# A stick-breaking and a softmax attention loop: values stationary, output turned, gate turned, probabilities scaled by GpSimd

## Chip, core and metric

One NeuronCore of a Trainium2 chip runs the whole program. The metric is the device time of one execution in microseconds; the median of three runs stands for a kernel. TensorE, VectorE (DVE), ScalarE (ACT), GpSimd (POOL) and SyncE (SP) each work through a queue of their own and wait for each other through semaphores.

## What is computed

Two transformer blocks on 256 tokens of 1024 features, all in float32. The first has a pooling mixer (layer 0) and a stick-breaking attention with 16 heads of 64 (layer 1); the second has a layer with 8 MLA heads (96-wide keys, 64-wide values) and 8 MoBA heads of 64 that here are plain causal softmax, an S5 layer, and two squared-ReLU MLPs. The parts that matter:

```
# stick-breaking attention, heads of 64, mask s < t
logits   = q k^T / 8
log_keep = where(mask, log_sigmoid(-logits), 0)
later    = reverse_cumsum(log_keep) - log_keep
a        = where(mask, exp(log_sigmoid(logits) + later), 0)
o        = a v
x        = x + (o * silu(z)) @ b_w_out        # q, z = split(rms_norm(x) @ b_w_in)
# softmax attention, 16 heads, mask s <= t
p        = softmax(where(mask, q k^T, -inf))
x        = x + concat_heads(p v) @ w_o
```

## The kernel before

Tokens lie on the partitions in two tiles of 128 (`NT` = 2). A dense product needs both operands with the contracted features on the partitions, so `turn` transposes activations on TensorE (L728) into `hT`, and each float32 factor is split into a high part and a low rest: ScalarE writes the high part (`turned_high`, `whi` in `fill`), VectorE the low part (`turned_low`, `wlo` in `fill`). A product is three matmuls per block of 128 features (`three`, L735 to L737): activations stationary, 512 columns of weights moving. The MLP of layer 0 has it the other way round (`hidden`, L1060 to L1064): weights stationary, 256 token columns moving.

Weights come through a ring of two blocks, loaded by SP in the order of `loads`; SP waits for `low_made` of the block two before. They are split in halves of 128 x 2048 into three parts of `whi` and `wlo`; `refill(name, half)` in the queues of ScalarE and VectorE makes the half that stands three halves behind `name`.

The eight banks of PSUM are given out by a plan written by hand (`plan`, `soft_plan`): each use of a bank is a unit with the engine that empties it ("a" ScalarE, "v" VectorE). `begin(unit)` makes TensorE wait until the previous unit of that bank is emptied. Each engine's queue is written out in the order of the code; nothing is scheduled at run time.

Layer 1 runs its products in the order `k`, `v`, `q`, `zb` (the gate z), with the turns of k and q between them. `v`, `q`, `k` and the gate lie token by token (`v_tok` and so on); the gate is scaled by the rows' `rstd` and put through Silu by ScalarE as it leaves PSUM (L1281).

The stick loop goes over pairs of heads, j = 0 to 10, with `LAG` = 2. In iteration j TensorE does `stick_logits(j)` (L885 to L891, two heads on 64-row tiles), at j = 2 three products `ple` (L844), then `stick_logs` of pair j-2 (L898 to L903: the reverse cumulative sum as products with triangular matrices, added into the bank that holds the logits), then `stick_values` of pair j-3 (L912 to L914: the weights of a head as the stationary operand, 64 columns of values moving). `logits` and `loga` of head i use bank i % 6. ScalarE does, head by head, Abs (L1465), Exp (L1466), the Exp of the finished log weights (L1473) and Ln (L1480), each on 128 x 384. VectorE does softplus (L2085), the high part (L2090) and the low part (L2094) of it, and multiplies each four heads' output by the gate (L2100, into `h`). After the loop come `ple(1, 1, 1)`, the turn of `h` (unit "o1"), ScalarE's and VectorE's split of it, and the product `b_out`.

The softmax loop goes over i = 0 to 19 with `AHEAD` = 3. TensorE computes the scores of head i (`mla_scores`, L978 and L979; `moba_scores` for two heads at once, L992 and L994; the masks L968 and L969), turns the probabilities of head i-3 (`probs_turned`, L1003) and multiplies those of head i-4 with the values (`soft_values`, L1014 to L1016). VectorE does the maxima (L2209, L2210), copies the turned probabilities (L2229), and for each four heads the reciprocals of the sums and the scaling of the output (`soft_out`, L2217 and L2218); four pieces of the weights' low part (`refill_piece`, L1739) stand in its queue for i = 10 to 13. ScalarE does the two Exp of a head with their sums (L1537, L1539). The turned keys and queries of the MoBA heads come through bank 7. After the loop come the turn "o2" of `h`, its split, and the product `w_o`. GpSimd does nothing in this loop; behind it, it clears and stores `taps` and begins the S5 multiplies (L2425 to L2430).

## Time and profile before

| | us |
|---|---|
| median of three runs | 868.62 (868.02 to 869.25) |
| span of the profiled execution, first to last instruction | 866.2 |
| its own whole time | not on the page; the span is the figure to compare |
| TensorE busy | 851.7 (98% of the span), 5659 instructions |
| weight loads of TensorE | 737.0 (85%) |
| VectorE busy | 591.9 (68%) |
| ScalarE busy | 441.4 (51%) |
| GpSimd busy | 117.3 (14%) |
| granted TensorE clock | 1.000 over the whole span |

Durations of matmuls overlap (their ends are modelled), so the distance between starts is what a matmul costs, not its duration. A float32 product shows as two records, a product of split parts as one. The chain that ended last names what the end waited for at each moment; 2% of idle time of TensorE is spread over many short waits.

### The profile page before, as it was taken

To read this page: it belongs to the slowest core of one execution; us is meant where nothing else is said; L and a number is where in the kernel's file an instruction comes from. 1 tells how busy PE (TensorE), PEld (TensorE's weight loads), DVE (VectorE), ACT (ScalarE), POOL (GpSimd) and SP (SyncE) were. 2 spreads that over 40 slices of the span, in tenths; PEclk is the share of its full clock that TensorE was granted. 3 is DMA by queue.
4 is the path that set the end of the run, shared out by engine and by line. 5 is a ranking of instruction groups with operands and counts; after the bars stand their busy time and mean duration, and the time that the engine had idled before them with its cause. 6 is when DMAs were issued, how large, how long until landed. Compare 5 with 4: busy or idle time off the path is not lost.

```text
span 866.2 us, 13480 instructions
## 1 busy us (share of the span) xinstructions
PE 851.7 (98%) x5659; PEld 737.0 (85%) x5659; DVE 591.9 (68%) x738; ACT 441.4 (51%) x591; POOL 117.3 (14%) x74
## 2 busy tenths in 40 slices
PE   8999999999999999999999999999989999999998
PEld 7887888888788887888988889997868999999996
DVE  5684677666756678888788788786975655555553
ACT  6644466556953656754553446443164644444441
POOL 0100001111000004123144344540000000000000
PEclk9999999999999999999999999999999999999999
DMA  9927645555004436226455565556976465555621
GB/s 332 372 75 246 239 146 196 194 194 184 11 22 154 160 98 244 97 97 210 157 198 167 207 231 195 209 190 140 282 265 235 151 210 182 188 190 194 194 98 48
DMA packets 68405, 155.96 MB, mean 180 GB/s; under 512 B 3145, under 2 KB 6954, under 8 KB 68346
## 3 DMA queue, kind: packets, MB, share of 16 engines
q1 hardware_dynamic: 65312, 146.80, 50.1%
q0 software_dynamic: 2224, 7.67, 2.6%
q10 hardware_dynamic: 810, 0.63, 0.5%
q8 instruction: 45, 0.74, 0.3%
q14 instruction: 14, 0.11, 0.0%
HBM read 146.70 MB, written 7.34 MB: 178 GB/s over the span
## 4 chain that ended last, share of the span: by engine, by line
PE 91%; DVE 6%; ACT 2%; issue 1%; DMA 0%; ACTq 0%; DVEq 0%
PE bank L735 19%; PE bank L736 19%; PE bank L737 19%; PE bank L1062 7%; PE bank L1064 7%; PE bank L1060 7%; PE bank L728 3%; PE bank L844 2%; PE bank L834 1%; PE bank L946 1%; PE bank L885 1%; DVE pT L1826 1%; PE bank L1133 1%; PE bank L1122 1%; DMA vrows<-in_vecs 0%
## 5 line engine op out<-in xcount | busy, mean ns | idle before, releaser
L1725 DVE TENSOR_TENSOR wlo<-ring,whi 128x2048 fp32r<-128x2048 f32 (+1 forms) x103 | 251.7, 2449 | 135.3 <-ACT whi L1334 135.0
L1334 ACT ACTIVATE whi<-ring 128x2048 fp32r<-128x2048 f32 (+1 forms) x104 | 198.4, 1909 | 208.3 <-PE bank L737 143.2
L735 PE MATMUL bank<-whi,hT 128*128 128x512 f32 (+1 forms) x512 | 201.6, 394 | 3.2 <-DVE wlo L1955 1.4
L737 PE MATMUL bank<-whi,hT 128*128 128x512 f32 (+1 forms) x512 | 198.8, 388 | 0.0
L736 PE MATMUL bank<-wlo,hT 128*128 128x512 f32 (+1 forms) x512 | 198.7, 388 | 0.0
L1060 PE MATMUL bank<-hT,whi 128*128 128x256 f32 x512 | 145.3, 284 | 0.0
L1062 PE MATMUL bank<-hT,whi 128*128 128x256 f32 x512 | 144.9, 283 | 0.0
L1064 PE MATMUL bank<-hT,wlo 128*128 128x256 f32 x512 | 144.8, 283 | 0.0
L735 PEld LDWEIGHTS bank<-whi,hT 128*128 128x128 f32 x512 | 96.1, 188 | 25.0 <-issue 2.7
L737 PEld LDWEIGHTS bank<-whi,hT 128*128 128x128 f32 x512 | 96.1, 188 | 19.6
L736 PEld LDWEIGHTS bank<-wlo,hT 128*128 128x128 f32 x512 | 96.2, 188 | 19.0 <-issue 0.5
L1060 PEld LDWEIGHTS bank<-hT,whi 128*128 128x128 f32 x512 | 98.2, 192 | 0.6
L1062 PEld LDWEIGHTS bank<-hT,whi 128*128 128x128 f32 x512 | 98.2, 192 | 0.5
L1064 PEld LDWEIGHTS bank<-hT,wlo 128*128 128x128 f32 x512 | 98.2, 192 | 0.0
L735 PE MATMUL bank<-whi,hidT_hi 128*128 128x512 f32 x224 | 88.0, 393 | 0.0
L736 PE MATMUL bank<-wlo,hidT_hi 128*128 128x512 f32 x224 | 87.4, 390 | 0.0
L737 PE MATMUL bank<-whi,hidT_lo 128*128 128x512 f32 x224 | 87.2, 389 | 0.0
L1720 DVE SCALAR_TENSOR_TENSOR wlo<-ring,vcols,whi 128x512 fp32r<-128x512 f32 x64 | 43.8, 745 | 20.6 <-ACT whi L1330 20.6
L1330 ACT ACTIVATE whi<-ring,vcols 128x512 fp32r<-128x512 f32 x64 | 40.9, 711 | 19.3 <-PE bank L737 17.0
L735 PEld LDWEIGHTS bank<-whi,hidT_hi 128*128 128x128 f32 x224 | 42.1, 188 | 9.7 <-issue 1.2
L737 PEld LDWEIGHTS bank<-whi,hidT_lo 128*128 128x128 f32 x224 | 42.1, 188 | 9.0
L736 PEld LDWEIGHTS bank<-wlo,hidT_hi 128*128 128x128 f32 x224 | 42.1, 188 | 8.2
(296 smaller groups left out, 1026.9 us busy)
## 6 DMA issues: line engine op xcount, KB each, us to landing
ring<-in_w_ff SPq DMA_DIRECT2D x64, 1024.0 KB, 5.3
ring<-in_ple_gate_w SPq DMA_DIRECT2D x8, 1024.0 KB, 5.0
ring<-in_w_kv SPq DMA_DIRECT2D x8, 1024.0 KB, 5.0
ring<-in_b_w_in SPq DMA_DIRECT2D x8, 1024.0 KB, 5.0
ring<-in_a_w_in SPq DMA_DIRECT2D x7, 1024.0 KB, 13.1
ring<-in_w_in SPq DMA_DIRECT2D x6, 1024.0 KB, 5.8
ring<-in_w_glu SPq DMA_DIRECT2D x6, 1024.0 KB, 10.1
ring<-in_a_w_out SPq DMA_DIRECT2D x4, 1024.0 KB, 5.7
```

The source lines that it names most:

```text
L728: last = pe.transpose(b[0:width, cc * S + t * P:cc * S + t * P + P], src[:, t, c * width:(c + 1) * width], ident)
L735: pe.matmul(bank_cols, high[:, at[0], at[1]], w_high, start=first, stop=False)
L736: pe.matmul(bank_cols, high[:, at[0], at[1]], w_low, start=False, stop=False)
L737: return pe.matmul(bank_cols, low[:, at[0], at[1]], w_high, start=False, stop=last)
L844: last = pe.matmul(b[:, :], pT[:, l, k, t * P:(t + 1) * P], ple_rows[:, k, nb * 512:(nb + 1) * 512], start=(k == 0), stop=(k == 1))
L1060: pe.matmul(b[:, at:at + S], w_high[:, kk, cols], hT_hi[:, k, :], start=k == 0 and at == 0, stop=False, skip_group_check=True)
L1062: pe.matmul(b[:, at:at + S], w_high[:, kk, cols], hT_lo[:, k, :], start=False, stop=False, skip_group_check=True)
L1064: last = pe.matmul(b[:, at:at + S], w_low[:, kk, cols], hT_hi[:, k, :], start=False, stop=k == KC - 1, skip_group_check=True)
L1330: ins = act.activation(whi[at][:, n], ring[:, slot[name], cols][:, n], ACT.Copy, scale=gain(gained[name[0]], 4 * (g % 2) + kk))
L1334: act.activation(whi[at], raw_rows(g), ACT.Copy).then_inc(high_made, 1)
L1720: ins = dve.scalar_tensor_tensor(out=wlo[at][:, n], in0=ring[:, slot[name], cols][:, n], scalar=gain(gained[name[0]], 4 * (g % 2) + kk), i ...
L1725: dve.tensor_tensor(wlo[at], raw_rows(g), whi[at], ALU.subtract).then_inc(low_made, 1)
```

## The change

- `v` is computed after the gate: products in the order `k`, `q`, `zb`, `v`, and the weights are loaded in that order.
- The gate comes out turned (`turned_product`): weights stationary, `hT` moving, features on the partitions. The rows' `rstd` are now needed along the columns, so VectorE makes two diagonal matrices (`diag`) and TensorE multiplies them by a constant matrix of -1 (`rows_of_rstd`, unit "rows"); VectorE scales the gate by them as it leaves PSUM (`z_out`) and ScalarE applies Silu in place (`silu_of_z`).
- Stick loop: `stick_values` takes a pair of heads, the values (128 x 64) stationary and the weights moving (256, then 128 columns), the two heads on column tiles 0 to 63 and 64 to 127. The output is turned, so "o1" goes: VectorE multiplies by the turned gate into `oz`, ScalarE and VectorE split it (`oz_split`, `oz_low`). ScalarE's and VectorE's operations of the loop take both heads of a pair at once, over two banks (`bank_pair`).
- Softmax loop: `soft_values` likewise for pairs. The output can't be scaled by a column of reciprocals any more, so VectorE takes the reciprocals head by head (`reciprocals`) and GpSimd scales the probabilities in place, two operations a head, before TensorE turns them. "o2" is no turn any more; its units hold the values' output and are split inside the loop.

```diff
@@ plan and loads
-    gemm(u, "v", 2, "a")
+    for t in range(NT):
+        u.add(("q", 0, t), "a")
+    u.add("rows", "v")
+    for t in range(NT):
+        u.add(("q", 1, t), "a")
     turned(u, "k")
-    gemm(u, "q", 2, "a")
-    gemm(u, ("zb", 0), 1, "a")
+    gemm(u, ("zb", 0), 1, "v")
...
+    for nb in range(2):
+        for t in range(NT):
+            u.add(("v", nb, t), "a", bank=2 + 4 * nb + t)
...
-            u.add(("soft_out", m), "v", bank=6 + m % 2)
+            u.add(("T", "o2", m), "av", bank=6 + m % 2)
@@ TensorE
+            def rows_of_rstd():
...
+                for t in range(NT):
+                    last = pe.matmul(b[:, t * P:(t + 1) * P], allneg[:, :], diag[:, t, :], start=True, stop=True)
+            def turned_product(name, between=None):
...
+                    for c in range(4):
...
+                        for kk in range(4):
+                            k = 4 * half + kk
+                            pe.matmul(to, w_high[:, kk, cols], hT_hi[:, k, :], start=k == 0 and at == 0, stop=False,
+                                      skip_group_check=True)
...
-            def stick_values(n):
+            def stick_values(c):
...
+                emptied(("loga", 2 * c + 1))
+                sides = []
+                for odd in range(2):
+                    n = 2 * c + odd
+                    sides.append((b[HD * odd:HD * odd + HD, at:at + S], v_tok[:, :, n * HD:(n + 1) * HD], sticks[:, n % 4, :]))
+                for o, vh, a in sides:
+                    pe.matmul(o, vh[:, 0, :], a[:, 0:S], start=True, stop=False, skip_group_check=True)
+                for o, vh, a in sides:
+                    last = pe.matmul(o[:, P:S], vh[:, 1, :], a[:, S:384], start=False, stop=True, skip_group_check=True)
...
             def probs_turned(n):
-                emptied(("scores", n))
+                pe.wait_ge(probs_scaled, 2 * n + 2)
...
-                if i > AHEAD:
-                    soft_values(i - AHEAD - 1)
+                if i > AHEAD and (i - AHEAD) % 2 == 0:
+                    soft_values((i - AHEAD) // 2 - 1)
...
-            turn("o2", h, ready=lambda k: emptied(("soft_out", k)))
@@ ScalarE, stick loop
+                    filled(("logits", 2 * j + 1))
+                    if j >= 2:
+                        act.wait_ge(sp_ready, j - 1)
+                    act.activation(logs[:, two, :], bank_pair("logits", j), ACT.Abs).then_inc(abs_ready, 1)
+                    act.wait_ge(abs_ready, j + 1)
+                    act.activation(logs[:, two, :], logs[:, two, :], ACT.Exp, scale=-1.0).then_inc(exps_ready, 1)
+                if j >= LAG:
+                    c = j - LAG
+                    filled(("loga", 2 * c + 1))
+                    act.activation(sticks[:, 2 * (c % 2):2 * (c % 2) + 2, :], bank_pair("loga", c), ACT.Exp)\
+                        .then_inc(act_emptied, 2)
+                if j < NH // 2:
+                    act.wait_ge(exps_ready, j + 1)
+                    act.activation(logs[:, two, :], logs[:, two, :], ACT.Ln, bias=1.0).then_inc(logs_ready, 1)
@@ VectorE, softmax loop
+            def reciprocals(i):
+                n, head = divmod(i, MH)
+                emptied(("scores", i))
+                dve.reciprocal(rden[:, n, head, :], den[:, n, head, :]).then_inc(rden_ready, 1)
...
+                if 0 < i <= 2 * MH:
+                    reciprocals(i - 1)
+                if i in (9, 13, 17):
+                    turned_low("o2", None, ((i - 9) // 4,))
@@ GpSimd
+            for i in range(2 * MH):
+                n, head = divmod(i, MH)
+                pool.wait_ge(rden_ready, i + 1)
+                for t, cols in enumerate((slice(0, P), slice(P, 384))):
+                    a = probs[:, i % 3, cols]
+                    pool.tensor_scalar(a, a, rden[:, n, head, t:t + 1], None, ALU.mult).then_inc(probs_scaled, 1)
```

## Rows read from the trace of the kernel before

**Rows 1.** The page, part 4: the chain that ended last, by engine

```profile
PE 91%; DVE 6%; ACT 2%; issue 1%; DMA 0%; ACTq 0%; DVEq 0%
```

**Rows 2.** Timeline of TensorE, stick loop: start, duration (us), line, operands, count, wait

```profile
213.13 0.70 PE L885 MATMUL bank<-work 64*128 64x256 f32 x4
...
223.73 0.70 PE L885 MATMUL bank<-work 64*128 64x256 f32 x4 [0.63 <-ACT aux L1473]
...
226.02 0.33 PE L912 MATMUL bank<-work,aux 128*128 128x64 f32 x2
...
231.06 0.70 PE L885 MATMUL bank<-work 64*128 64x256 f32 x4
```

**Rows 3.** Timeline of ScalarE, stick loop

```profile
222.57 1.06 ACT L1473 ACTIVATE aux<-bank 128x384 f32<-128x384 f32 x2 [0.90 <-PE bank L903]
...
229.25 0.53 ACT L1466 ACTIVATE aux<-aux 128x384 f32<-128x384 f32 x1
229.69 0.85 ACT L1473 ACTIVATE aux<-bank 128x384 f32<-128x384 f32 x2
230.43 0.49 ACT L1465 ACTIVATE aux<-bank 128x384 f32<-128x384 f32 x1
...
232.24 0.49 ACT L1465 ACTIVATE aux<-bank 128x384 f32<-128x384 f32 x1
```

**Rows 4.** Timeline of TensorE, end of the stick stage

```profile
248.33 1.94 PE L844 MATMUL bank<-ple_rows,pT 128*128 128x512 f32 x4
250.11 1.91 PE L728 MATMUL bank<-cst,h 128*128 128x128 f32 x16
252.32 0.47 PE L735 MATMUL bank<-whi,hT 128*128 128x512 f32 x1 [0.31 <-DVE hT L1708]
```

**Rows 5.** Timeline of TensorE, softmax stage: first scores, three MoBA pairs, first `w_o` product

```profile
352.48 0.39 PE L978 MATMUL bank<-work 96*128 96x128 f32 x2
...
370.15 0.49 PE L992 MATMUL bank<-pT,sig 64*128 64x128 f32 x4
...
373.28 0.49 PE L992 MATMUL bank<-pT,sig 64*128 64x128 f32 x4
...
377.30 0.49 PE L992 MATMUL bank<-pT,sig 64*128 64x128 f32 x4
...
386.81 0.47 PE L735 MATMUL bank<-whi,hT 128*128 128x512 f32 x1
```

**Rows 6.** Timeline of VectorE, softmax stage

```profile
372.33 0.68 DVE L1739 TENSOR_TENSOR wlo<-ring,whi 128x512 fp32r<-128x512 f32 x1
372.93 0.28 DVE L2209 TENSOR_REDUCE nmax<-bank 128x1 f32<-128x128 f32 x1
...
373.46 0.54 DVE L2229 COPY aux<-bank 128x384 f32<-128x384 f32 x1
373.93 0.19 DVE L2217 RECIPROCAL rden<-den 128x8 f32<-128x8 f32 x1
```

**Rows 7.** Busy time by stretch: PE, PEld, DVE, ACT, POOL, clock, DMA share, GB/s

```profile
174.00:184.00 10.00, 10.00 (x46) 8.29 (x45) 4.73 (x8) 5.84 (x10) 0.00 (x0) 1.00 0.55 201
414.00:424.00 10.00, 10.00 (x85) 10.00 (x84) 7.65 (x10) 7.09 (x10) 0.00 (x0) 1.00 0.49 148
```

**Rows 8.** Timeline of TensorE, S5 stage: products on 32-column tiles

```profile
615.72 1.95 PE L1200 MATMUL bank<-spare,work 128*32 128x128 f32 x64
```

**Rows 9.** Groups by line: ScalarE's widest operation (busy us, mean ns, idle before)

```profile
L1334 ACT ACTIVATE whi<-ring 128x2048 fp32r<-128x2048 f32 (+1 forms) x104 | 198.4, 1909 | 208.3 <-PE bank L737 143.2 <-PE bank L1064 38.4 <-DMA ring<-in_w_in 10.8
```

**Rows 10.** Groups by line: GpSimd's elementwise operations

```profile
L2425 POOL TENSOR_TENSOR aux<-pa,cs 128x1152 f32<-128x1152 f32 x4 | 10.5, 2619 | 69.5 <-PE bank L1064 69.5
L2410 POOL COPY sig<-fade 128x1024 f32<-128x1024 f32 x1 | 1.7, 1658 | 0.0
```

**Rows 11.** Timeline of VectorE: the same low part with GpSimd idle, and with it multiplying

```profile
346.82 2.28 DVE L1725 TENSOR_TENSOR wlo<-ring,whi 128x2048 fp32r<-128x2048 f32 x1
...
389.43 5.06 DVE L1725 TENSOR_TENSOR wlo<-ring,whi 128x2048 fp32r<-128x2048 f32 x1 [0.79 <-ACT whi L1334]
```

More of the change, by code:

```diff
@@ L277, in soft_plan @@
             u.add(("T", name, k), "a", bank=7)
+    for m in range(3):
+        u.freed_in_order([("probsT", 4 * m + 5), ("probsT", 4 * m + 6), ("T", "o2", m)])
 def hidden_bank(layer, i):
@@ L403, in sem @@
             return ctx.enter_context(nc.semaphore(name))
[L405 removed]
+        bank_all = ctx.enter_context(nc.psum_tensor("bank", [P, 8 * 512], F32))
+        ps = [bank_all[:, 512 * i:512 * i + 512] for i in range(8)]
         x = sb("x", [P, NT, D])
@@ L864, in _ @@
             out_and_gate(0, "a_out", "mixed")
-            for stage in ("k", "v"):
-                for nb in range(2):
-                    product(stage, nb, (stage, nb), turned_by="kv" if stage == "k" else None, first=(
-                        lambda: turn("kv", x, units=(2, 3), ready=x_gated(0))) if (stage, nb) == ("k", 0) else None)
+            def rows_of_rstd():
+                b = begin("rows")
+                pe.wait_ge(diag_ready, NT)
+                for t in range(NT):
+                    last = pe.matmul(b[:, t * P:(t + 1) * P], allneg[:, :], diag[:, t, :], start=True, stop=True)
+                last.then_inc(pe_done, 1)
@@ new lines, in turned_product @@
+            def turned_product(name, between=None):
+                banks = [begin((name, 0, n)) for n in range(2)]
+                for half in range(2):
+                    g = 2 * order[name] + half
+                    w_high, w_low = part_views(g, 4, 512)
+                    pe.wait_ge(low_made, g + 1)
+                    for c in range(4):
+                        cols = slice(c * P, (c + 1) * P)
+                        at = S * (c % 2)
+                        to = banks[c // 2][:, at:at + S]
+                        for kk in range(4):
+                            k = 4 * half + kk
+                            pe.matmul(to, w_high[:, kk, cols], hT_hi[:, k, :], start=k == 0 and at == 0, stop=False,
+                                      skip_group_check=True)
+                            pe.matmul(to, w_high[:, kk, cols], hT_lo[:, k, :], start=False, stop=False,
+                                      skip_group_check=True)
+                            last = pe.matmul(to, w_low[:, kk, cols], hT_hi[:, k, :], start=False, stop=k == KC - 1,
+                                             skip_group_check=True)
+                        if half and c % 2:
+                            last.then_inc(pe_done, 1)
+                        elif half == 0 and c == 3:
+                            last.then_inc(first_used, 1)
+                    if between and half == 0:
+                        between()
@@ L871, in _ @@
+            for nb in range(2):
+                product("k", nb, ("k", nb), turned_by="kv", first=None if nb else (
+                    lambda: turn("kv", x, units=(2, 3), ready=x_gated(0))))
+            product("q", 0, ("q", 0))
+            rows_of_rstd()
+            product("q", 1, ("q", 1))
             turn("k", k_tok, ready=lambda k: pe.wait_ge(heads_normed, 1 + k // 2))
+            turned_product(("zb", 0))
+            turned_product(("zb", 1),
+                           between=lambda: turn("q", q_tok, ready=lambda k: pe.wait_ge(heads_normed, 3 + k // 2)))
```

242 lines of the change are left out of this document (125 added, 117 removed).

## The prediction

> **What bounds the kernel now.** I read the chain that ended last first: TensorE is 91% of it [rows 1]. So the question is not how long an operation lasts, but whether TensorE runs fewer microseconds of work, or waits more, in the two attention stages. Everything outside them (feeds of weights, MLPs, S5) keeps its instructions and its order, so I give it nothing.
>
> Then the timeline of TensorE in the stick loop [rows 2]. One pair of heads takes 3.67 us: two periods lie between the `stick_logits` starts at 223.73 and 231.06. In a period TensorE does logits, `stick_logs` and, from 226.02, the two heads' values, up to 227.4 (223.73 + 3.67): 1.38 us for twelve records with 64 columns and a change of tiles, 0.11 a record. The same loop on ScalarE [rows 3]: Exp of one head at 229.25, the Exp of two heads' log weights at 229.69, the next Abs at 230.43; with two Abs, two Exp and two Ln of some 0.45 beside the 0.74, ScalarE needs 3.5 us for a pair. So the loop has two nearly equal limits. From the first logits (213.13) to the first `b_out` product (252.32) the stage takes 39.19 us [rows 2, 4], with the turn of the output in it at 250.11.
>
> The softmax stage lasts from 352.48 to 386.81, 34.33 us [rows 5]. Its pairs of MoBA heads begin at 370.15, 373.28 and 377.30: 3.13 us where TensorE leads, 4.02 where VectorE has refill pieces in its queue. VectorE's share of one head is a maximum (0.53), a piece of `wlo` (0.60), a copy (0.47) [rows 6].
>
> **The gate products.** `zb` changes from 2 x 48 matmuls with 512 moving columns to 2 x 96 with 256. In a stretch of the old form 10 us hold 46 records, two of them only reaching in, 0.227 us each; in a stretch of the turned form (L1060 to L1064, the same three factors) they hold 85, 0.120 each [rows 7]. 192 x 0.120 less 96 x 0.227 is +1.2 us, all on TensorE, which has no gap there. `rows_of_rstd` adds two f32 products, four records of 128 columns: +0.4 (0.3 to 0.6). That `v` moves behind `zb` costs nothing, nor do the four `z_out` on VectorE: in the stretch of products TensorE is busy for 10.00 of 10 us, ScalarE for 5.84 and VectorE for 4.73 [rows 7], so the feed has four free microseconds in ten for some 0.7 us a bank, and SP's loads keep their distance of two blocks from the splits. If that cover is gone, a late half costs about its low part, 2.3 us [rows 11].
>
> **The stick loop.** TensorE's values become two column tiles of 64: 256 and then 128 moving columns each. In one stretch 64 records of 128 columns on 128*32 tiles take 1.95 us [rows 8], 0.03 each, where a record of only 64 columns takes 0.11 in the full form [rows 2]; so column tiles run side by side. An f32 record of 512 columns lasts 0.44 (four in the 1.78 us from 248.33 to 250.11 [rows 4]), so 384 columns in two records are 0.66 for both heads together; with 0.1 for a change of tiles (1.38 less twelve times 0.11 leaves 0.06) a pair costs 0.75 to 0.80 us instead of 1.34. Bounds: 0.66, and 1.32 if nothing overlaps. The Trainium skill (TensorEngine Tiling (Array Packing), Key Properties) adds that a change of tiling mode drains the engine. By that rule each change costs something; nothing in the sum hangs on it.
>
> But these 0.55 us a pair are not what ends the wait. `logits` of pair j go to the banks of `loga` of pair j-3, and ScalarE empties these now by one operation that stands behind Abs(j-1) and Exp(j-1), both twice as wide. The handover can already be seen once: TensorE idle 0.63 us at 223.73 until ScalarE's operation of 222.57 [rows 2, 3]. The new cycle, step by step: logits start to ScalarE 1.18 us for the first bank (231.06 to 232.24), 1.28 for the second, which Abs now waits for; Abs of 768 columns, priced between 384 columns (0.49) and 2048 (1.91) [rows 3, 9]: 0.82; Exp 0.75 to the next start (0.44 for 384, 229.25 to 229.69, plus 384 columns at 0.83 ns); the Exp of the log weights 0.82; handover 0.10 (222.57 + 1.06 to 223.73). Sum 3.77 us against 3.67: TensorE's gain turns into its wait. Bounds for a wide operation: two narrow ones without a wait between them (0.74) and with all their length (0.98); the cycle is then 3.5 to 4.2. I take the slope, as both ends of it are operations of this kind.
>
> Five pairs (j = 3 to 7) go by this cycle; the start of j = 7 is late by 0.6 us. The tail is shorter. Before, from that start (238.41, four periods after 223.73) to `b_out` 13.9 us. After: 1.28, Abs, Exp, log-weight Exp and Ln (together 3.2), VectorE's softplus, split and low part for two heads (2.5), the last `stick_logs` (0.8), Exp (1.0), values (0.8), `ple` (1.76): 11.4. The turn (1.75) and its wait (0.31) are gone; `oz` of the last quarter is late by some 3 us behind the first `b_out` product, which reads it only in its second half, 5.4 us in. Stage: +0.6 - 2.5, **-1.8 us**.
>
> **The softmax loop.** The turn of `o2` goes, sixteen transposes and a wait like those from 250.11 to 252.32: 2.2 us [rows 4]. Values cost 0.80 a pair instead of 1.34. GpSimd gets two operations a head (128 and 256 columns). Nearest row: a copy of 1024 columns in 1.66 us [rows 10], so 384 columns and two starts are about 0.8 us. Bounds: well below that nothing changes, since it is hidden under three heads of lead; above, the two-input product there, 2.6 us for 1152 columns or 2.3 ns a column, gives 0.9 and with waits 1.4. I take the copy, which like this one reads one tensor.
>
> Each head now has exp, reciprocal on VectorE (0.19 long for eight columns [rows 6]; I count 0.1 of its queue and 0.26 to GpSimd), 0.8 GpSimd, transposes. In the first eight heads this eats most of what the values save (gain 0.2). In the MoBA part the values of a pair stand only one set of transposes behind the copy that they need: scores to VectorE 1.18, maxima 0.53, copy 0.59, values 0.80, change of tiles 0.1: 3.2 us a pair, against 3.13, twice. The pair with pieces is VectorE's: 2 x (0.53 + 0.47 + 0.10 + 0.60) = 3.4, say 3.5, against 4.02. From the last scores (377.30) to `w_o` 9.5 us; after: maxima of head 15 done at 3.7, exp 1.0, reciprocal 0.3, GpSimd 0.9, transposes 0.5, copy 0.6, values 0.8, and about 0.5 of queueing: 8.3. Sum -0.2 + 0.1 - 0.5 - 1.2 = -1.8; I keep 0.3 back for tile changes in all eight pairs: **-1.5 us**. `turned_low` (0.69 a quarter) stands in VectorE's queue where `soft_out` stood with its reciprocal; the last quarter is hidden under the first half of `w_o`.
>
> One more contention shows: with GpSimd multiplying at the same time VectorE's `wlo` of 2048 columns took 5.06 us, alone 2.28 [rows 11]. Here four refill pieces meet the GpSimd scaling, some 0.45 us of delay for each of four heads; GpSimd has that slack at 0.8 us a head. The Trainium skill (SBUF — State Buffer, Who interferes with whom) says that a VectorE operation with two SBUF inputs and a GpSimd one that reads SBUF exclude each other for their whole length; the row agrees.
>
> **Sum.** +1.2 + 0.4 - 1.8 - 1.5 = -1.7 us. The span of the profile is 866.2; the median of the runs is 868.62, 2.4 more, which lies around the span and stays. Predicted 868.62 - 1.7 = **866.9 us**. What a measurement of this kernel can tell is about 0.2%, 1.74 us; the forecast stands on that edge.
>
> **Rivals.**
> (A) My forecast: TensorE's savings become waits, the turns are the gain. Its own range, from the bounds of the ScalarE widths (cycle 3.5 to 4.2 over five pairs, -1.3 to +2.1) and half a microsecond either way in the softmax stage: 865.1 to 869.5. Chance 0.55; the edge of 0.2% cuts it in two: 0.27 faster, 0.28 same.
> (B) The look-ahead holds and TensorE keeps its pace in both loops: stick pairs 3.1 us, five times 0.57 less than before, with the turn gone -2.9 - 2.1; softmax eight pairs 0.54 less and 2.2 of turn, -6.5 less what VectorE's pieces take, -5: 868.62 + 1.6 - 5.0 - 5.0 = 860. For it: three heads of lead in both loops. Against: the wait at 223.73, and the bank order. Chance 0.14, half-way cases with it.
> (C) Slower: GpSimd's scaling becomes the bound of the softmax loop. It starts its first head 3.7 us into the stage and has 16 in a row; behind the last come 1.9 us of transposes, copy and values. At 2.0 us a head the stage is 3.7 + 32 + 1.9 = 37.6 us, +3.3 instead of -1.5: 868.62 + 1.6 - 1.8 + 3.3 = 871.7. It decides from 1.7 us a head (3.7 + 27.2 + 1.9 = 32.8, my stage) and passes the 0.2% at 1.9. For it: no row shows a multiply by a column of scalars on GpSimd, and the waits [rows 11]. Against: the plain rows. Chance 0.16, 0.13 of it beyond the edge.
> (D) The column tiles don't overlap, or the gate products starve on a late half: values 1.28 us a pair, stick stage -1.0, softmax +0.5: 868.62 + 1.6 - 1.0 + 0.5 = 869.7, and up to 2.7 more with a late half. Against: [rows 8]. Chance 0.15, 0.07 of it slower.
>
> The rule that speaks most against the change stands in the Trainium skill (TensorEngine Tiling (Array Packing), PSUM Bottleneck): tiling speeds TensorE, and the emptying of PSUM may bind instead. As a mechanism of this kernel it is (A).
>
> Together: faster 0.27 and 0.14; same 0.28, 0.03 and 0.08; slower 0.13 and 0.07. That is 0.41, 0.39, 0.20. The range goes from (B)'s half-way cases at 863.3 to (C) with 1.9 us a head at 871.0.
>
> **What would show it.** Between starts of `stick_logits` 3.7 to 3.9 us for j = 4 to 7, with TensorE idle about 0.6 us before each, released by ScalarE; values about 0.8 us a pair; `zb` halves 5.75 us; no turn before `b_out` and `w_o`; GpSimd's two operations together 0.8 us; MoBA pairs 3.2 to 3.5 apart. A stick period near 3.1, or idle TensorE in the products, or transposes released by GpSimd through the whole softmax loop, would make it wrong.

## The result and the profile after

The changed kernel takes **877.61 us** (median of 4 runs, 876.74 to 879.63) against 868.38 us for the kernel before on the same chip: ratio **1.0111, interval 1.0098 to 1.0125**. By the ratio it is slower by 9.6 us, where the forecast was 866.9, faster by 1.7; the range ended at 871.0. In what follows the gain of an edit is the difference of such ratios, each taken against runs of the kernel before on the same chip, with 0.1% for 0.87 us. One ratio is uncertain by some 0.13%, so a difference of two by about 0.19% or 1.6 us; smaller gains rest on the stages of the traces. One of the twelve runs of `all_mended` below took 1695.42 us for a reason that no trace shows; its median counts it, its ratio does not.

First the chain that ended last, of the kernel after. In [rows 1] TensorE holds 91% of it; now it holds less, and GpSimd, which was not in it at all, is there with 2%:

```profile
PE 83%; DVE 9%; ACT 4%; POOL 2%; issue 1%; DMA 0%; ACTq 0%; DVEq 0%
```

So TensorE waits more. To find where, I set the two traces side by side at points that both have: a turn of `x` at 124.25 and 124.71 (all before it is the same work, and there the thirteen profiles of changed kernels lie between 124.14 and 125.24, so the 0.46 us are taken as no effect), the first `stick_logits`, the first `b_out` product, the first softmax scores, the MoBA pairs, the first `w_o` product, the first product of the MLP. The spans differ by 875.5 - 866.2 = 9.3 us:

| stretch | before | after | difference | forecast |
|---|---|---|---|---|
| up to the turn at 124 | 124.25 | 124.71 | +0.46 | 0 |
| from there to the first stick logits | 88.88 | 93.74 | **+4.86** | +1.6 |
| stick stage, to the first `b_out` product | 39.19 | 37.32 | -1.87 | -1.8 |
| `b_out` to the first scores | 100.16 | 100.55 | +0.39 | 0 |
| softmax, first eight heads | 14.53 | 15.50 | +0.97 | -0.2 |
| softmax, first to last MoBA pair | 10.29 | 10.56 | +0.27 | -0.4 |
| softmax, last pair to `w_o` | 9.51 | 10.92 | **+1.41** | -1.2 |
| `w_o` to the first MLP product | 22.78 | 25.14 | **+2.36** | 0 |
| from there to the end | 456.61 | 457.06 | +0.45 | 0 |

(The +0.39 belongs to the stick stage: the first `b_out` record begins at 255.77 under the last `ple` one and lasts 0.80.) The bold rows hold 8.6 of the 9.3 us, and the forecast had 0.4 for them together.

**The products.** Timeline of TensorE after, and below it VectorE and GpSimd in the same stretch (start, duration, line, operation, operands, count, idle time and its releaser):

```profile
155.34 0.39 PE L755 MATMUL bank<-whi,hT 128*128 128x512 f32 x1
158.61 0.68 PE L892 MATMUL bank<-sig,allneg 128*128 128x128 f32 x4 [2.88 <-DVE sig L2137]
159.05 0.48 PE L753 MATMUL bank<-whi,hT 128*128 128x512 f32 x1
```

```profile
153.31 2.73 DVE L1800 SCALAR_TENSOR_TENSOR wlo<-ring,vcols,whi 128x512 fp32r<-128x512 f32 x4
156.85 1.23 DVE L2122 TENSOR_TENSOR work<-work,rsh 128x1024 f32<-128x1024 f32 x1 [0.81 <-POOL rsh L2487]
157.99 0.48 DVE L2137 TENSOR_SCALAR sig<-cst,rstd 128x128 f32<-128x128 f32 x2
```

```profile
153.48 3.33 POOL L2487 TENSOR_TENSOR rsh<-msh,half_neg 128x16 f32<-128x16 f32 x1 [7.54 <-DVE msh L2116]
```

`rows_of_rstd` (L892) stands in TensorE's queue behind the first block of `q`, which ended near 155.7, and reads two diagonal matrices that VectorE makes at 157.99. They need nothing but `rstd`, which GpSimd had made by 131. But in VectorE's queue they stand behind a low part of 2.73 us, then 0.81 us of waiting for GpSimd's operation of 3.33 us (the power that makes `rsh`), then `half_scale`. TensorE stands for 2.88 us, and with it the second block of `q`. The rest of this row is what was forecast: 0.44 from the start of `rows_of_rstd` to the next product, and `zb` from 171.72 to 196.57 with one turn of 1.75 in it, 23.1 us or 192 x 0.120.

**The stick loop.** Timeline of TensorE, starts of `stick_logits` from the sixth pair on, and ScalarE in one cycle:

```profile
236.98 0.70 PE L941 MATMUL bank<-work 64*128 64x256 f32 x4 [0.52 <-ACT aux L1551]
...
239.36 0.65 PE L975 MATMUL bank<-aux,work 128*64 128x256 f32 x4
...
240.75 0.70 PE L941 MATMUL bank<-work 64*128 64x256 f32 x4 [0.52 <-ACT aux L1551]
...
244.53 0.70 PE L941 MATMUL bank<-work 64*128 64x256 f32 x4 [0.52 <-ACT aux L1551]
```

```profile
238.27 0.81 ACT L1545 ACTIVATE aux<-bank 128x768 f32<-128x768 f32 x1 [0.66 <-PE bank L947]
239.11 0.85 ACT L1547 ACTIVATE aux<-aux 128x768 f32<-128x768 f32 x1
239.86 0.79 ACT L1551 ACTIVATE aux<-bank 128x768 f32<-128x768 f32 x1
240.55 0.83 ACT L1555 ACTIVATE aux<-aux 128x768 f32<-128x768 f32 x1
```

The cycle is 3.77 us, the figure of the forecast, and by its steps: logits at 236.98, Abs at 238.27, Exp at 239.11, log weights at 239.86, and TensorE's next logits 0.89 us behind that. What the column tiles save returns as 0.52 us of idle time a pair (the values of a pair take 0.80 us, from 246.92 to 247.72).

**The softmax loop.** GpSimd's groups by shape (busy us, mean ns | idle before), then from the timelines four heads of GpSimd in the MoBA pairs and three in the tail, and the transposes (L1064) of three heads on TensorE:

```profile
L2500 POOL TENSOR_SCALAR aux<-aux,rden 128x256 f32<-128x256 f32 x16 | 15.0, 937 | 0.0
...
L2500 POOL TENSOR_SCALAR aux<-aux,rden 128x128 f32<-128x128 f32 x16 | 10.5, 658 | 4.3 <-DVE rden L2318 4.1
```

```profile
377.47 7.20 POOL L2500 TENSOR_SCALAR aux<-aux,rden 128x128 f32<-128x128 f32 x8 [0.24 <-DVE rden L2318]
385.04 4.46 POOL L2500 TENSOR_SCALAR aux<-aux,rden 128x128 f32<-128x128 f32 x6 [0.37 <-DVE rden L2318]
```

```profile
384.81 0.52 PE L1064 MATMUL bank<-cst,aux 128*128 128x128 f32 x3 [0.83 <-POOL aux L2500]
...
386.68 0.52 PE L1064 MATMUL bank<-cst,aux 128*128 128x128 f32 x3 [0.56 <-POOL aux L2500]
...
388.17 0.52 PE L1064 MATMUL bank<-cst,aux 128*128 128x128 f32 x3 [0.96 <-POOL aux L2500]
```

Six operations in 4.46 us are three heads, **1.49 us a head**, where the forecast had 0.8 and 1.4 as its upper bound; the transposes of the last heads follow at just this distance (386.68 to 388.17). The four heads from 377.47 take 7.20 us, **1.80 us a head**; in this stretch VectorE makes its four pieces of `wv`. Eight of the sixteen transposes wait for GpSimd, 4.95 us in all.

**The output of the softmax.** TensorE and VectorE where `w_o` begins, then TensorE where the MLP begins:

```profile
391.36 0.42 PE L1082 MATMUL bank<-aux,work 128*64 128x128 f32 x4
393.30 0.76 PE L753 MATMUL bank<-whi,hT 128*128 128x512 f32 x1 [1.52 <-DVE hT L1788]
393.86 0.63 PE L754 MATMUL bank<-wlo,hT 128*128 128x512 f32 x1
...
418.44 0.36 PE L1125 MATMUL bank<-hT,whi 128*128 128x256 f32 x1 [0.86 <-DVE x L1836]
```

```profile
392.44 0.76 DVE L1788 SCALAR_TENSOR_TENSOR hT<-bank,hT 128x256 fp32r<-128x256 f32 x2 [1.68 <-ACT hT L1368]
```

The first product of `w_o` reads only the first quarter of the output, ready since 375.9; yet it waits for VectorE's low part of the **last** quarter. The reason is not in the data but in the banks. The planner deals banks in turn. The change takes twelve units out of the turn ahead of `w_o` (four of `v`, which now has fixed banks, four of "o1", four of "o2") and puts one in ("rows"): eleven fewer, which on eight banks is a shift by three. So `w_o` is dealt banks 6 and 7, where before it had 1 and 2, and 7 is the bank from which the last quarter is read. The wait stands before the first product, because `product` claims the banks of both token tiles before it starts. Its second column block is dealt 2 and 3, which the first MLP block takes by a fixed rule, so this waits 0.86 us for the last addition to `x` at 418.44. And TensorE came to `w_o` with a clock that had fallen (columns: stretch, length, busy time of PE, PEld, DVE, ACT, POOL, granted clock, DMA share, GB/s):

```profile
382.38:388.00 5.62, 3.44 (x31) 2.13 (x29) 4.25 (x15) 3.02 (x13) 5.25 (x8) 1.00 0.53 164
388.00:393.30 5.30, 2.71 (x22) 1.71 (x23) 2.54 (x6) 1.49 (x2) 2.66 (x5) 0.95 0.07 28
393.30:396.30 3.00, 3.00 (x7) 2.39 (x8) 2.06 (x1) 0.91 (x1) 2.98 (x5) 0.52 0.75 273
```

In the tail it was busy for 6.15 of 10.92 us; then for 3 us it gets about half of its clock, 1.2 GHz for most of them: 7 products where at full speed, 0.227 apart, 13 would have stood. That is most of the other 1.5 us of the 2.36.

### The profile page after: what moved, and what is told of

Read it like the earlier page. It is cut to its first block, busy times and chain, and to the rows that moved or that the text cites. A ratio compares the mean times of both kernels' runs of the same rounds, so it can differ in the third digit from the quotient of the medians.

```text
span 875.5 us, 13469 instructions
## 1 busy us (share of the span) xinstructions
PE 847.6 (97%) x5663; PEld 727.4 (83%) x5663; DVE 589.1 (67%) x725; ACT 439.2 (50%) x559; POOL 141.2 (16%) x106
## 4 chain that ended last, share of the span: by engine, by line
PE 83%; DVE 9%; ACT 4%; POOL 2%; issue 1%; DMA 0%; ACTq 0%; DVEq 0%
PE bank L753 17%; PE bank L754 16%; PE bank L755 16%; PE bank L1125 7%; PE bank L1129 7%; PE bank L1127 7%; PE bank L746 2%; PE bank L864 2%; DVE wlo L1805 1%; PE bank L908 1%; PE bank L912 1%; PE bank L910 1%; POOL aux L2500 1%; POOL rsh L2493 1%; PE bank L854 1%
## 5 line engine op out<-in xcount | busy, mean ns | idle before, releaser
L1805 DVE TENSOR_TENSOR wlo<-ring,whi 128x2048 fp32r<-128x2048 f32 (+1 forms) x103 | 247.9, 2411 | 143.0 <-ACT whi L1399 142.8
L753 PE MATMUL bank<-whi,hT 128*128 128x512 f32 (+1 forms) x480 | 190.3, 396 | 4.2 <-DVE hT L1788 1.5
L755 PE MATMUL bank<-whi,hT 128*128 128x512 f32 (+1 forms) x480 | 187.1, 390 | 0.0
L754 PE MATMUL bank<-wlo,hT 128*128 128x512 f32 (+1 forms) x480 | 187.0, 390 | 0.0
L753 PEld LDWEIGHTS bank<-whi,hT 128*128 128x128 f32 x480 | 90.6, 189 | 25.0 <-issue 2.4
L755 PEld LDWEIGHTS bank<-whi,hT 128*128 128x128 f32 x480 | 90.4, 188 | 18.4
L754 PEld LDWEIGHTS bank<-wlo,hT 128*128 128x128 f32 x480 | 90.6, 189 | 18.1 <-issue 0.7
## 6 DMA issues: line engine op xcount, KB each, us to landing
ring<-in_a_w_in SPq DMA_DIRECT2D x7, 1024.0 KB, 11.3
```

Of the source, the lines that this page charges most:

```text
L753: pe.matmul(bank_cols, high[:, at[0], at[1]], w_high, start=first, stop=False)
L754: pe.matmul(bank_cols, high[:, at[0], at[1]], w_low, start=False, stop=False)
L755: return pe.matmul(bank_cols, low[:, at[0], at[1]], w_high, start=False, stop=last)
L1805: dve.tensor_tensor(wlo[at], raw_rows(g), whi[at], ALU.subtract).then_inc(low_made, 1)
```

## The experiments

Two theories stood against each other. **Mine:** the time went into four named waits (diagonals, GpSimd's rate, the banks of `w_o`, ScalarE's order), each of which goes when its cause goes. **The rival:** such a wait only covers the next limit (VectorE's queue, the feed of weights, the tiles), and mending it gives little. Every edit is made to the kernel after, with all else as it is.

**1. The diagonals early** (`diag_early`)

```diff
             half_scale(k_tok, 0)
+            dve.wait_ge(rstd_ready, 2)
+            for t in range(NT):
+                dve.tensor_scalar(diag[:, t, :], ident, rstd[:, 1, t:t + 1], None, ALU.mult).then_inc(diag_ready, 1)
             refill(("k", 1), 1)
...
             half_scale(k_tok, 1)
-            dve.wait_ge(rstd_ready, 2)
-            for t in range(NT):
-                dve.tensor_scalar(...).then_inc(diag_ready, 1)
```

> Theory (waits): the whole of the 2.9 us that TensorE stands before rows_of_rstd comes from the two diagonal operations standing in VectorE's queue behind half_means(k, 1), refill(q, 0) and a half_scale that waits for GpSimd's power. Put behind half_scale(k, 0), where VectorE is idle for 0.86 us in the profile of the change, they cost nothing: the wait goes, the first stick logits come 2.9 us earlier, and the kernel takes 877.6 - 2.9 = 874.7 us. Rival (the wait only moves): the stall also lets the feed of weights catch up, so that with it gone a product behind it (q 1 or zb) waits for a low part instead; then less than 1 us is won, 876.6 or more.

Measured: 873.79 us, ratio 1.0061 [1.0048, 1.0074], so 0.50% or 4.3 us of the 9.6. TensorE of this kernel:

```profile
154.77 0.40 PE L755 MATMUL bank<-whi,hT 128*128 128x512 f32 x1
155.00 0.61 PE L892 MATMUL bank<-sig,allneg 128*128 128x128 f32 x4
155.37 0.48 PE L753 MATMUL bank<-whi,hT 128*128 128x512 f32 x1
...
214.74 0.49 PE L941 MATMUL bank<-work 64*128 64x256 f32 x2
```

From its turn of `x` at 124.14 to the first logits at 214.74 it takes 90.60 us, +1.72 on before, where the forecast had +1.6: no other wait took its place, and the feed did keep up with `v` behind `zb`. The rival is out. But 4.3 us are more than the 3.1 that this stretch is shorter. The clock can give a reason. In the profiles of four of the eight kernels that have the wait (the change itself not among them) it falls behind it; this is `banks_as_before` and then `diag_early` in the same stretch:

```profile
160.00:165.00 5.00, 5.00 (x15) 3.91 (x14) 4.40 (x7) 0.00 (x0) 0.46 (x1) 0.56 0.52 166
```

```profile
160.00:165.00 5.00, 5.00 (x24) 4.14 (x23) 4.93 (x8) 3.26 (x5) 0.88 (x1) 1.00 0.58 174
```

At clock 0.56 the stretch from the turn to the first logits is 96.48 us instead of 93.74. So the wait costs 3.1 us when the clock holds (93.74 against 90.60) and 6.0 at most when it falls (96.58, `scaling_of_256`), and an idle stretch of one length can do either. That this makes up the rest of the 4.3 is not shown: the profile of the change is one in which the clock held, and its other executions have no trace.

**2. The banks of `w_o` as before** (`banks_as_before`): three more in the turn, which with the eleven makes no shift on eight banks.

```diff
     soft_plan(u)
+    u.turn += 3
     rolled(u, "w_o", ("ffn", 0), "v")
```

> Theory (banks): with turned_in_two gone from the plan the banks of w_o rotate by four, onto the bank of the last quarter of the softmax output (bank 7) and, at the other end, onto the banks that the first MLP block takes (2 and 3). With the banks of the kernel before, w_o starts when its first quarter is there: the 1.52 us idle before it mostly go, the 0.86 us idle before the first MLP block go, and some of the 1.4 us that the first ten w_o products lose at the low clock: 877.6 - 2.4 = 875.2 us, down to 873.8 if the clock stays up as well. Rival: w_o waits for the same quarter through the high part on ScalarE or its low parts of weights all the same, and only the 0.86 go: 876.7.

Measured: 874.27 us, ratio 1.0066 [1.0052, 1.008], 0.45% or 3.9 us. Every engine runs the same operations in the same order; only bank numbers differ, and the waits that hang on them. Where `w_o` begins, and the MLP:

```profile
393.96 0.42 PE L1083 MATMUL bank<-aux,work 128*64 128x128 f32 x4
394.31 0.50 PE L754 MATMUL bank<-whi,hT 128*128 128x512 f32 x1
394.64 0.40 PE L755 MATMUL bank<-wlo,hT 128*128 128x512 f32 x1
...
417.14 0.28 PE L1126 MATMUL bank<-hT,whi 128*128 128x256 f32 x1
```

Both waits are gone, and the second product lasts 0.40 us instead of 0.63. The tail is 9.32 us (10.92), `w_o` takes 22.83 (25.14): 3.9 us, as measured. The clock stays up as well: without the last 1.52 us of idle time it does not fall. My expectation left that open, between 2.4 and 3.8. It also laid the shift to "o2" alone; those four units by themselves would have put `w_o` on banks 5 and 6.

**3. Without the division** (`no_scaling`)

```diff
             def probs_turned(n):
-                pe.wait_ge(probs_scaled, 2 * n + 2)
+                emptied(("scores", n))
...
-            for i in range(2 * MH):
-                n, head = divmod(i, MH)
-                pool.wait_ge(rden_ready, i + 1)
-                for t, cols in enumerate((slice(0, P), slice(P, 384))):
-                    a = probs[:, i % 3, cols]
-                    pool.tensor_scalar(a, a, rden[:, n, head, t:t + 1], None, ALU.mult).then_inc(probs_scaled, 1)
```

> The probabilities are not divided by their sums here (GpSimd's 32 multiplications are left out, the reciprocals stay). Theory (GpSimd is late): at 1.49 us a head and one head at a time it sets the tail, where TensorE waits 0.56 to 0.96 us for it four times, and half of the waits before: the softmax stage falls from 36.98 to some 32.5 us, and the low clock at w_o goes with the idle time: 877.6 - 4.5 - 1 = about 872 us. Rival (GpSimd is only the last to be seen; VectorE's queue or the column tiles are the limit): the waits go over to the copies, and less than 1.5 us is won, 876 or more.

**4. Only 256 of 384 columns divided** (`scaling_of_256`): GpSimd's operation on the first 128 is left out.

> The first 128 columns of each head stay undivided (0.55 us a head of GpSimd left out, nothing put in its place on VectorE); all else as in the change. Theory (GpSimd's time a head is the price): between the 36.98 us of the softmax stage at 1.49 us a head and 33.89 at none; the tail has four heads one behind the other, 4 x 0.55 = 2.2 less until the latency of the chain takes over: stage 34.6 us, kernel 875.6. Rival (only doing nothing on GpSimd helps, since its handover of 0.3 to 0.4 us stays): stage 36.0 or more, 876.8.

Measured: 875.55 us, 1.0079 [1.0066, 1.0093], and 876.95 us, 1.0088 [1.0071, 1.0105]. The stages give the dose and its effect better than the totals:

| | heads 1 to 8 | MoBA pairs | tail | stage | gain |
|---|---|---|---|---|---|
| after (1.49 us a head, 1.80 beside pieces) | 15.50 | 10.56 | 10.92 | 36.98 | |
| 256 columns (0.92, beside pieces 1.28) | 14.52 | 9.98 | 10.01 | 34.51 | 2.5 |
| none | 14.40 | 9.75 | 9.74 | 33.89 | 3.1 |

I expected 34.6 for the second (right; the kernel 875.6) and 32.5 for the third (the kernel about 872), where I had missed that the chain of exp, transposes, copy and values takes over. In both, `w_o` still waits 1.52 us for its bank and begins at a clock of about 0.5 (its stretch is 25.25 and 25.18 us). So GpSimd costs 3.1 us in all, and four fifths of it come from the 128 columns more: its rate is the price, not the handover. The rival had its part too: with no division at all TensorE waits 4.5 us in all before `soft_values` for VectorE's copies, where the change has 1.2.

**5. The softmax loop as before** (`softmax_as_before`): its plan units, `soft_out`, values, turn and division as in the kernel before, with the banks that `w_o` had there; products and stick loop of the change.

```diff
     soft_plan(u)
+    u.turn += 7
+    turned_in_two(u, "o2")
     rolled(u, "w_o", ("ffn", 0), "v")
...
+            turn("o2", h, ready=lambda k: emptied(("soft_out", k)))
             for nb in range(2):
                 product("w_o", nb, ("w_o", nb), turned_by="o2", between=(
```

> The softmax loop, its turn, its division and the banks of w_o as before; gate products, stick loop and all else as in the change. Theory: of the 9.3 us the softmax stage with w_o and its banks holds 2.7 (stage) + 1.4 (low clock) + 0.9 (bank wait) + 0.3, the products and the stick stage together 5.3 - 1.5 = 3.8: 877.6 - 5.2 = 872.4 us. Rival (the memory layout, one PSUM tensor, or the reordered loads cost something later): it stays above 874.

Measured: 873.1 us, ratio 1.0055 [1.0042, 1.0068]: 0.56% or 4.9 us. The expected time was 872.4. Its stages are 14.54, 10.29, 9.51 and 22.75, those of before to 0.03. The change is two changes with two separate prices: 4.9 us here and the rest in products and stick loop.

**6. The division on another engine.** `split_scaling`: VectorE divides 128 columns behind its reciprocal, GpSimd 256. `scaling_on_vector`: VectorE does both.

```diff
                 dve.reciprocal(rden[:, n, head, :], den[:, n, head, :]).then_inc(rden_ready, 1)
+                a = probs[:, i % 3, 0:P]
+                dve.wait_ge(rden_ready, i + 1)
+                dve.tensor_scalar(a, a, rden[:, n, head, 0:1], None, ALU.mult).then_inc(first_scaled, 1)
...
-                for t, cols in enumerate((slice(0, P), slice(P, 384))):
-                    a = probs[:, i % 3, cols]
-                    pool.tensor_scalar(a, a, rden[:, n, head, t:t + 1], None, ALU.mult).then_inc(probs_scaled, 1)
+                a = probs[:, i % 3, P:384]
+                pool.tensor_scalar(a, a, rden[:, n, head, 1:2], None, ALU.mult).then_inc(probs_scaled, 1)
```

> VectorE scales the first 128 columns of each head (right behind its reciprocal), GpSimd the other 256 (0.94 us). Theory (GpSimd's 1.49 us a head set the waits of the tail and of the pairs with pieces): a head costs GpSimd 0.94 instead of 1.49; the four waits on it in the tail lose about 0.5 each, the MoBA part some 0.5: 877.6 - 2.0 = 875.6 us, close to the kernel that leaves the scaling out (875.6). Rival (VectorE's queue is as near a limit): its additional 0.15 to 0.2 a head in the queue takes it back, 877 or more.

> GpSimd does nothing in the softmax loop; VectorE does both multiplications of a head behind its reciprocal, an estimated 0.35 us a head (a 128-column copy and the reciprocal take 0.15 to 0.2 in its queue). Theory (what costs is latency and GpSimd's rate, not VectorE's load): first eight heads as without scaling (14.4), tail 9.9 to 10.2; pairs with pieces of wv now VectorE's, 3.9 instead of 3.7: 877.6 - 1.6 = 876.0 us. Rival (VectorE bound): its loop becomes 1.45 us a head and 2.05 with a piece, the MoBA pairs cost 0.5 more, and nothing is won: 877.5.

Measured: 876.57 us, 1.0094 [1.008, 1.0109], a gain of 0.17% or 1.5 us, within the uncertainty; and 883.34 us, 1.0168 [1.0155, 1.0182], a loss of 0.57% or 5.0 us. The second misses by 7 us, and one stretch shows how; VectorE of `scaling_on_vector`:

```profile
378.00 0.16 DVE L2318 RECIPROCAL rden<-den 128x2 f32<-128x2 f32 x1
378.20 0.55 DVE L2322 TENSOR_SCALAR aux<-aux,rden 128x128 f32<-128x128 f32 x2
378.66 0.68 DVE L1819 TENSOR_TENSOR wlo<-ring,whi 128x512 fp32r<-128x512 f32 x1
379.26 0.28 DVE L2312 TENSOR_REDUCE nmax<-bank 128x1 f32<-128x128 f32 x1
```

From the reciprocal to the next operation are 0.66 us, 0.12 of them the engine waiting for its own result, against 0.07 in the change. From this head's reciprocal to the next one's at 380.26 are 2.26 us, where I had 2.05; the stage becomes 41.35 us. Of the 4.4 us on the change 0.5 lie in the first eight heads, 1.1 in the pairs and 2.8 in the tail, which with 13.68 us ran at a mean clock of 0.71; what of these 2.8 is VectorE's queue and what is clock was not separated. VectorE is the second limit of this loop, as the rival said, though at 877.5 the rival missed the size too. The profile of `split_scaling` shows a tail of 13.13 us at a clock of 0.67, but it is of an execution of 881.33 us, where the median is 876.57, and does not stand for it.

GpSimd's operation of 256 columns in `split_scaling` shows the two engines in each other's way. It takes 1.54 us where VectorE makes a low part from two tensors in SBUF at the same time (378.87), and 1.02 where it does not:

```profile
378.73 1.54 POOL L2505 TENSOR_SCALAR aux<-aux,rden 128x256 f32<-128x256 f32 x1 [1.04 <-DVE rden L2321]
...
388.75 1.02 POOL L2505 TENSOR_SCALAR aux<-aux,rden 128x256 f32<-128x256 f32 x1 [0.37 <-DVE rden L2321]
```

The Trainium skill (SBUF — State Buffer, Who interferes with whom) says that such a VectorE instruction contends with a GpSimd one that reads SBUF, and that the order of issue decides who blocks. The rows agree that the two meet, but not on the order: GpSimd's record begins 0.14 us before VectorE's, and yet it is GpSimd's that grows, by 0.5 us, while VectorE's piece lasts 0.69 us, as with an idle GpSimd (0.68 in the stretch above). In `scaling_of_256`, where VectorE's piece begins first (378.70, GpSimd's at 378.88), GpSimd's takes 1.28 us, which fits the order. In the change itself the same meeting shows as the 1.80 us a head of the four heads from 377.47.

**7. ScalarE's order in the stick loop** (`stick_order`)

```diff
                     act.activation(logs[:, two, :], bank_pair("logits", j), ACT.Abs).then_inc(abs_ready, 1)
-                    act.wait_ge(abs_ready, j + 1)
-                    act.activation(logs[:, two, :], logs[:, two, :], ACT.Exp, scale=-1.0).then_inc(exps_ready, 1)
-                if j >= LAG:
+                early = LAG <= j < NH // 2 - 1
+                if early:
+                    log_weights(j - LAG)
+                if j < NH // 2:
+                    act.wait_ge(abs_ready, j + 1)
+                    act.activation(logs[:, two, :], logs[:, two, :], ACT.Exp, scale=-1.0).then_inc(exps_ready, 1)
+                if j >= LAG and not early:
+                    log_weights(j - LAG)
```

> ScalarE's Exp of the log weights goes between Abs and Exp of the new pair (but for the last). Theory (the order of ScalarE's queue makes the 3.77 us cycle: logits, Abs, Exp, log weights, handover): banks come free 0.75 us earlier, the cycle falls to what ScalarE needs, about 3.4 us, the 0.52 us idle before each pair of logits go: 5 x 0.4 = 2.0 us, 877.6 - 2.0 = 875.6 us. Rival (the new cycle goes through VectorE's softplus or the log weights, which come later): under 0.7 us is won, 877 or more.

Measured: 877.48 us, ratio 1.0099 [1.0086, 1.0112], 0.12% or 1.0 us: between the two. Its timeline, TensorE and then ScalarE:

```profile
237.43 0.70 PE L941 MATMUL bank<-work 64*128 64x256 f32 x4 [0.21 <-ACT aux L1548]
...
240.90 0.70 PE L941 MATMUL bank<-work 64*128 64x256 f32 x4 [0.21 <-ACT aux L1548]
```

```profile
238.84 0.80 ACT L1545 ACTIVATE aux<-bank 128x768 f32<-128x768 f32 x1
239.99 0.81 ACT L1548 ACTIVATE aux<-bank 128x768 f32<-128x768 f32 x1 [0.35 <-PE bank L959]
240.70 0.83 ACT L1555 ACTIVATE aux<-aux 128x768 f32<-128x768 f32 x1
```

The cycle falls from 3.77 to 3.46 us, which confirms that the order of ScalarE's queue made it. The gain in time is within the uncertainty; this cycle and the stage are what shows it. What is left is ScalarE's own: four operations of 0.7 to 0.85 and 0.35 us in which it now waits for `stick_logs`. The gain comes four times, not five: the fourth pair (j = 3) waits 1.01 us for its banks as in the change. The stage is 36.23 us (37.32).

**8. Put together.** `all_mended` has edits 1, 2 and 7 and the split of the division; `three_mended` has 1, 2 and 7 alone; `vector_unloaded` adds to it the low part of the second quarter and the last piece of `wv` behind the last maxima; `softmax_before_mended` is number 5 with edits 1 and 7.

> The change with the diagonals early, the banks of w_o as before, the scaling split between VectorE and GpSimd, and the new order of ScalarE in the stick loop. If the gains add (3.8 and 3.3 measured, 2.0 and 2.0 expected): 877.6 - 11.1 = 866.5 us, faster than both kernels. Rival (they overlap: the tail is shortened twice over, and the feed of weights falls behind): 868 to 870.

> The change with the diagonals early, the banks of w_o as before and the new order of ScalarE in the stick loop; GpSimd scales alone, as in the change. Theory (gains of different stages add: 3.8, 3.3 and about 1.1 measured): 877.6 - 8.2 = 869.4 us, or 0.5 less than the kernel with the split scaling if VectorE's extra operation and the low clock in its tail cost more than GpSimd's 0.55 us a head: 868.3 us, level with the kernel before. Rival (the split was worth something): 870 or more.

> As three_mended, with the low part of the second output quarter two heads later and the last piece of wv three heads later, behind the last maxima. Theory (the last maxima stand behind these two in VectorE's queue, 1.26 us): the last two heads reach ScalarE up to 0.6 us earlier, GpSimd's row of heads begins so much earlier, the tail is 0.3 to 0.6 us shorter: 0.4 us below three_mended. Rival (GpSimd's rate alone sets the tail: it is busy from 377.5 to 384.7 in the profile of the change without a break): no difference, within 0.2 us.

> Softmax loop, turn and division as before; stick loop and gate products of the change, with the diagonals early and the new order of ScalarE. Against the kernel before: products +1.7 (the 1.9 predicted), stick stage -1.5 - 1.1: in sum -0.9 us, 867.5 us if nothing else differs. Rival (the new stick part never pays): 868.5 or more.

| | median, us | ratio to before | stick stage | softmax stage | `w_o` |
|---|---|---|---|---|---|
| `all_mended` | 869.41 | 1.0014 [1.0003, 1.0026] | 36.22 | 35.84 | 22.85 |
| `three_mended` | 868.79 | 1.0006 [0.9997, 1.0015] | 36.23 | 35.40 | 22.83 |
| `vector_unloaded` | 868.86 | 1.0008 [0.9999, 1.0016] | 36.22 | 35.52 | 22.78 |
| `softmax_before_mended` | 867.78 | 1.0003 [0.9993, 1.0013] | 36.22 | 34.32 | 22.75 |

The gains add: 4.3 + 3.9 + 1.0 = 9.2 us against 9.1 (1.0111 less 1.0006) measured, and in the traces, from the turn to the first MLP product, 3.1 + 3.9 + 1.1 = 8.1 against 8.15 (293.73 less 285.58). So the loss of the change goes with three mended things. What is left of it comes to +0.2 us in that part (285.58 against 285.34): products +1.7, stick stage with the row of `b_out` -2.6, softmax stage +1.1. The softmax stage, with GpSimd's division in it, thus still costs more than before, and the stick stage pays for that. The split, which seemed to win 1.5 us alone, loses 0.4 us of stage when the rest is mended; its tail is 10.06 us at clock 0.83, against 9.32 at 1.00. Unloading VectorE did nothing (tail 9.44): GpSimd's row of heads has hardly a break from 373 to 385, as the rival had it, and the transposes of two heads now wait 0.59 and 0.49 us behind VectorE's low parts. No version beats the kernel before by more than can be measured. (The median of `softmax_before_mended` is 0.45 us below the 868.23 of the kernel before on that chip, but its times spread from 867.1 to 871.2 us, and the interval of its ratio holds 1.) Of `softmax_before_mended` I had expected -0.9 us; up to the first MLP product its trace has just this (284.41 us from the turn, 285.34 before), and behind it, in work that no edit touches, 457.8 us against 456.6. That last difference is not explained: short stops of TensorE in the S5 stage, marked "issue", come and go from profile to profile (1.18 and 1.04 us here), and this part takes between 456.7 and 457.8 us in the profiles of the changed kernels.

## Why the prediction was wrong

- **The gate products.** +1.2 for `zb` and the +0.4 that the records of the rows take on TensorE are right (1.72 in sum with the wait mended, 1.6 forecast), and so is the cover of the feed for `v`. What failed is the step "That `v` moves behind `zb` costs nothing, nor do the four `z_out`", which went over everything that moved except the two instructions that TensorE waits for. The term that failed is "+0.4 (0.3 to 0.6)" for `rows_of_rstd`: it is the price of its records on TensorE, and the wait for `diag` stands in it at nothing. I never asked when `diag` is ready: behind which instructions it stands on VectorE, and what these wait for. Cost: 3.1 us in the profiles where the clock held and up to 6.0 where it fell, 4.3 by the edit.
- **The stick loop.** Right, step by step: a cycle of 3.77 us, 0.52 us of idle time released by ScalarE (about 0.6 forecast), values 0.80 a pair, -1.5 us with the row of `b_out` against -1.8.
- **The softmax loop, GpSimd.** "I take the copy" was the wrong one of two rows: 384 columns and two starts were put at 0.8 us from a copy, the two-input product gave 0.9 to 1.4, and 1.49 was measured, above both. From start to start the operation of 128 columns takes 0.58 us and that of 256 takes 0.90 (385.04, 385.62, 386.52): 2.5 ns for each further column, near the 2.3 of the two-input product of [rows 10] and not the 1.6 of the copy, and some 0.26 us besides that each of the two operations pays. The bound was too narrow, since no row had the form. Beside the refill pieces four heads took 1.80 us, 0.31 more (0.45 forecast), and "GpSimd has that slack" did not hold. The mean of all sixteen is 1.57 us, under the "1.7 us a head" from which rival (C) decides, and the division cost 3.1 us all the same. That threshold counted GpSimd as a row of sixteen heads from the first to the last. But a head can be late without the sum being so: against the run with 256 columns, the first eight heads lose 1.0, the pairs 0.6 and the tail 0.9.
- **The softmax loop, the end.** "The last quarter is hidden under the first half of `w_o`" is true of the data and false of the bank. The diff showed `turned_in_two(u, "o2")` and two other groups leaving the turn; I priced the turns as work that goes and did not deal the banks again. Cost: 3.9 us by the edit, 1.6 in the tail and 2.3 in `w_o`. With the banks mended the stage is 35.4 us; without division it would be some 32.3 (an estimate, 33.9 less the 1.6, as the two edits were not made together). My 32.8 lies between these, where 0.8 us a head belongs.
- **The rivals.** (C) came nearest to what happened, by its engine though not by its size or sum; nothing that I listed had a product waiting for its bank. The range itself had a slip: by (C)'s own sum 1.9 us a head gives 870.1 us, not the 871.0 of its upper end, which takes nearly 2.0. The two missed terms and the mis-sized one are +4.3, +3.9 and +2.5 to 3.1: 866.9 + 10.7 to 11.3 is 877.6 to 878.2, and 877.6 was measured. That it closes so well is in part luck, since each of these gains is uncertain by about 1.6 us.

## What to carry to other kernels

When an operation is added on a busy engine, write down for each of its inputs which queue makes it and what stands ahead of it there; two operations of 0.24 us cost four microseconds by their place. When units join or leave a plan that deals buffers in turn, or are given fixed places, deal them all again on paper: who reads a buffer last and who takes it next is part of the diff, though no line of it says so. And allow idle time of TensorE more than its length: its clock can come down behind it, as in four of eight profiles here, and then the work behind it pays again.

## What the runs showed that I had not expected

- The clock does not fall after each such stop. One and the same stop of 2.88 us left the granted clock at 1.00 from 160 to 165 us in four kernels and at 0.56 to 0.85 in four; the stretch grew by up to 2.8 us. Behind a tail of 10.92 us, 6.15 of them busy and the last 1.52 idle, `w_o` began at a clock of 0.52; with the banks as before, behind 9.32 us with 6.07 busy, it began at 1.00.
- GpSimd's `tensor_scalar` with a column of scalars takes 0.90 us for 256 columns and 0.58 for 128, start to start: by the column about as much as its product of two tensors, although it reads one. Beside VectorE's products of two SBUF tensors one of 256 columns took 1.28 us (`scaling_of_256`) and 1.54 (`split_scaling`).
- VectorE takes 0.46 us for the same two multiplications, but with the reciprocal ahead of them, and 0.12 us in which they wait for its result, the three short operations hold its queue for 0.66 us.
